# PEER stage of a decoder step: selection from 65 instead of 256 sums, lookups in one instruction per rank, and other steps for the exponentials, the gathers and the spread

## The reference, cut to what matters

```python
s = jnp.einsum('thpd,hpkd->thpk', q, keys)                 # per token and head: two rows of 128 scores
sv, si = lax.top_k(s, 16)                                  # 16 best of each row, with their places
cand = sv[:, :, 0, :, None] + sv[:, :, 1, None, :]         # 16 x 16 sums
cv, ci = lax.top_k(cand.reshape(N, 8, 256), 16)            # the 16 best sums
i1 = jnp.take_along_axis(si[:, :, 0], ci // 16, axis=-1)   # back from ranks to keys
i2 = jnp.take_along_axis(si[:, :, 1], ci % 16, axis=-1)
eidx = i1 * 128 + i2
gate = jax.nn.softmax(cv, axis=-1)
h = gelu(einsum('tkd,td->tk', u_tab[eidx], x))
out = einsum('tk,tkd->td', gate * h, v_tab[eidx])
```

## Time and profile before

| | |
|---|---|
| median of 3 runs | 2303.91 us (2300.85 to 2310.2) |
| the profiled execution | 2299.57 us, span 2297.8 us, mean granted clock 0.946 |
| PE busy | 1972.6 us, 86% |
| DVE busy | 1512.0 us, 66% |
| ACT busy | 891.1 us, 39% |
| POOL busy | 784.5 us, 34% |
| HBM | 222 GB/s over the span |

### The profile page before, as it was taken

The page is one execution under the profiler, slowest core; times in us unless marked ns, Lnnn a source line. Parts: engine busy times, 40 slices in busy tenths (PEclk is TensorE's granted clock), DMA queues, the critical chain, the costliest instruction groups (busy, mean ns, idle before and its releaser), DMA issues. The chain is left out here.

```text
span 2297.8 us, 29795 instructions
## 1 busy us (share of the span) xinstructions
PE 1972.6 (86%) x11493; PEld 1785.1 (78%) x11493; DVE 1512.0 (66%) x2468; ACT 891.1 (39%) x1752; POOL 784.5 (34%) x440
## 2 busy tenths in 40 slices
PE   4999479848898898899899998777756999998998
PEld 3998479738797697799899997666645888777876
DVE  3676444271323212492799896999966888988888
ACT  2455112111422113333444343777753334433434
POOL 0233123012531023276576776333321222222221
PEclk9999689869999999999999998999988999999999
DMA  4221100022453313256699997789889999999996
GB/s 125 65 74 40 44 1 1 5 83 83 129 202 101 129 39 114 64 173 229 250 335 337 328 328 284 270 317 346 332 345 343 397 401 402 394 401 378 396 401 244
DMA packets 211501, 513.02 MB, mean 223 GB/s; under 512 B 13216, under 2 KB 143008, under 8 KB 174496
## 3 DMA queue, kind: packets, MB, share of 16 engines
q1 hardware_dynamic: 183712, 309.77, 39.0%
q0 software_dynamic: 27648, 201.34, 22.2%
HBM read 451.26 MB, written 59.80 MB: 222 GB/s over the span
## 5 line engine op out<-in xcount | busy, mean ns | idle before, releaser
L1557 POOL TENSOR_TENSOR ex_ulo<-ex_u,ex_uhi 128x1024 fp32r<-128x1024 f32 x128 | 324.5, 2540 | 312.8 <-ACT ex_uhi L1588 310.4
L1671 PE MATMUL ps<-xhi,ex_uhi 128*128 128x384 f32 x1024 | 356.0, 348 | 24.3 <-POOL ex_ulo L1557 18.7
L1671 PE MATMUL ps<-xhi,ex_ulo 128*128 128x384 f32 x1024 | 346.3, 338 | 0.0
L1671 PE MATMUL ps<-xlo,ex_uhi 128*128 128x384 f32 x1024 | 346.3, 338 | 0.0
L1951 PE MATMUL ps<-po_vhi,po_whi 128*128 128x512 f32 x768 | 239.4, 393 | 49.9 <-DVE po_wlo L1985 49.2
L1295 POOL DMA_INDIRECT ga_ring<-in_uv,ga_idx x138 | 171.7, 1244 | 292.0 <-DVE po_acc_s L1321 175.3
L1918 ACT CAST po_vhi<-po_v 128x1024 fp32r<-128x1024 f32 x128 | 133.8, 1047 | 327.7 <-DMA po_v<-in_peer_v 291.7
L1951 PE MATMUL ps<-po_vlo,po_whi 128*128 128x512 f32 x768 | 238.5, 392 | 0.0
L1951 PE MATMUL ps<-po_vhi,po_wlo 128*128 128x512 f32 x768 | 237.7, 391 | 0.0
L1671 PEld LDWEIGHTS ps<-xhi,ex_uhi 128*128 128x128 f32 x1024 | 195.4, 191 | 29.0 <-POOL ex_ulo L1557 22.7
L1951 PEld LDWEIGHTS ps<-po_vhi,po_whi 128*128 128x128 f32 x768 | 143.8, 189 | 84.0 <-issue 54.0
(11 more groups left out here) (379 smaller groups left out, 4205.4 us busy)
## 6 DMA issues: line engine op xcount, KB each, us to landing
ex_u<-in_uT SPq DMA_DIRECT2D x128, 512.0 KB, 5.6
po_v<-in_peer_v SPq DMA_DIRECT2D x64, 1024.0 KB, 10.4
acts<-ex_h SPq DMA_DIRECT2D x64, 384.0 KB, 3.0
gates<-scores SPq DMA_DIRECT2D x12, 2048.0 KB, 7.3
po_w<-acts SPq DMA_DIRECT2D x32, 768.0 KB, 12.7
po_g<-gates SPq DMA_DIRECT2D x32, 768.0 KB, 15.8
in_w_raw<-in_w_in SPq DMA_DIRECT2D x24, 512.0 KB, 4.0
at_cache<-in_cacheT SPq DMA_DIRECT2D x6, 1024.0 KB, 5.8
```

The source lines that it names most:

```text
L1557: pool.tensor_tensor(ulo[:, j % 3], u[:, j % 3], uhi[:, j % 3].bitcast(F32), ALU.subtract).then_inc(low, 1)
L1671: mm = pe.matmul(ps[:, j % 2, 0:ND], w[:, j % 3, k, :], x[:, k, :], start=(k == 0 and n == 0), stop=(k == KT - 1 and n == 2))
```

## The change

1. `FIRST_SPREAD` goes from 104 to 85, with three quads a step instead of four: the quads lie in steps 85 to 116 instead of 104 to 127. A pick comes after every third quad.
2. Steps 117 to 126 hold 20 more picks, two a step (`LATE`). So 100 picks are done in this block instead of 96, and 104 transfers are started in it instead of 103; three more are started at once when the output block begins.
3. The exponential of the gathered rows' gates goes from step 31 to step 19, the first seven transfers from step 26 to step 13, the picks 0 to 45 to one in 4/3 of a step from step 20. Picks 46 and 47 come after the last selection, at step 84. The exponential of the dense gates goes from step 104 to step 83.
4. A selection adds only the 65 sums that can be among the 16 best, into 72 places (five small additions and a memset), and searches those. The place in the 72 is turned into two ranks by shifts and multiplications with powers of two, and a rank into a key by 16 instructions on [128 x 128] (L1768), each comparing the ranks with one number and multiplying by that rank's place, and a sum over the 16 results, which lie 128 elements apart.
5. SP's stores of gates are at step `85 + 8 * (g + 1) // 3`, before at every second step.

```diff
-FIRST_SPREAD = 104
+FIRST_SPREAD = 85
+PER_STEP = 3
-LOOP_PICKS = EARLY + 2 * (NKEY - FIRST_SPREAD)
-def early_step(n):
-    return 31 + 3 * n // 2
+LATE = 20
+LOOP_PICKS = EARLY + QUADS // PER_STEP + LATE
+def pick_step(n):
+    if n < EARLY - 2:
+        return 20 + 4 * n // 3
+    if n < EARLY:
+        return FIRST_SPREAD - 1
+    if n < LOOP_PICKS - LATE:
+        return FIRST_SPREAD + n - EARLY
+    return FIRST_SPREAD + QUADS // PER_STEP + (n - LOOP_PICKS + LATE) // 2
...
         def _(sp):
-                g = (j - FIRST_SPREAD) // 2 - 1
-                if g >= 0 and j % 2 == 0:
-                    sp.wait_ge(spread_out, NG_QUADS * (g + 1))
-                    sp.dma_start(io["gates"][g], spread[g % 2]).then_inc(spread_stored, 16)
+                for g in range(ND // 32):
+                    if j == FIRST_SPREAD + NG_QUADS * (g + 1) // PER_STEP:
+                        sp.wait_ge(spread_out, NG_QUADS * (g + 1))
+                        sp.dma_start(io["gates"][g], spread[g % 2]).then_inc(spread_stored, 16)
...
         def _(pool):
-            for n in range(LOOP_PICKS + gather.SLOTS):
+            for n in range(LOOP_PICKS + 4):
                 before = n - gather.SLOTS
...
+                step = 13 if before < 0 else pick_step(min(before + 2, LOOP_PICKS - 1)) + 1
...
         def _(act):
-                if j == early_step(0):
+                if j == pick_step(0) - 1:
                     act.wait_ge(dropped, 1)
...
-                if j == FIRST_SPREAD:
+                if j == FIRST_SPREAD - 2:
                     act.wait_ge(dropped, 2)
                     act.activation(drops[:, :], drops[:, :], ACT.Exp).then_inc(exps, 1)
+                if j == FIRST_SPREAD:
                     scale(0)
+                for x in range(PER_STEP):
+                    q = PER_STEP * (j - FIRST_SPREAD) + x
+                    if 0 < q <= QUADS:
+                        evict(q - 1)
+                    if 0 <= q < QUADS - 1:
+                        scale(q + 1)
                 for n in at.get(j, []):
                     gather.weigh(act, n)
...
         def _(pe):
-                    if k % 2 and j >= FIRST_SPREAD:
-                        quad(4 * (j - FIRST_SPREAD) + k // 2)
+                    x = PER_STEP * (j - FIRST_SPREAD) + k // 2
+                    if k in (1, 3, 5) and 0 <= x < QUADS:
+                        quad(x)
...
         def _(dve):
-                after(dve.tensor_tensor(cand[:, 0:nh, :].rearrange("p h (a b) -> p h a b", a=TOPK),
-                                        last(b4[:, :, 0, :].unsqueeze(3), TOPK), over(b4[:, :, 1, :], 2, TOPK), ALU.add))
+                dve.memset(cand[:, 0:nh, 65:SLOTS], LOWEST)
+                for a0, na, nb, c0 in ((0, 1, 16, 0), (1, 2, 8, 16), (3, 4, 4, 32), (7, 8, 2, 48), (15, 1, 1, 64)):
+                    ins = dve.tensor_tensor(cand[:, 0:nh, c0:c0 + na * nb].rearrange("p h (a b) -> p h a b", a=na),
+                                            last(b4[:, :, 0, a0:a0 + na].unsqueeze(3), nb),
+                                            over(b4[:, :, 1, 0:nb], 2, na), ALU.add)
...
-                    after(dve.tensor_tensor(eq, last(partsf[:, q, 0:nj].unsqueeze(2), TOPK), over(iota16, 1, nj),
-                                            ALU.is_equal))
-                    after(dve.tensor_tensor(e4, e4, over(wheref[:, 0:nh, q, :], 2, TOPK), ALU.mult))
-                    after(dve.tensor_reduce(out[:, q, 0:nj], eq, AX, ALU.add))
+                    for x in range(TOPK):
+                        ins = dve.scalar_tensor_tensor(out=heads_of(lookup[:, x, 0:nj]), in0=heads_of(ranks[:, q, 0:nj]),
+                                                       scalar=float(x + 1 - q), in1=last(w4[:, :, q, x:x + 1], TOPK),
+                                                       op0=ALU.is_equal, op1=ALU.mult)
+                    after(ins)
+                    after(dve.tensor_reduce(out[:, q, 0:nj], lookup[:, :, 0:nj].rearrange("p a j -> p j a"), AX, ALU.add))
...
+            for n in range(EARLY - 2, EARLY):
+                pick(n)
...
-                if q % 2:
-                    pick(EARLY + q // 2)
+                if q % PER_STEP == PER_STEP - 1:
+                    pick(EARLY + q // PER_STEP)
+            for n in range(LOOP_PICKS - LATE, LOOP_PICKS):
+                pick(n)
```

More of the change, by code:

```diff
@@ L1493, in peer_experts @@
         where = sb("where", [P, 16, TOPK], U32)
-        wheref = sb("wheref", [P, PH, 2, TOPK])
-        cand = sb("cand", [P, PH, TOPK * TOPK])
+        lookup = sb("lookup", [P, TOPK, PICKS])
         top = sb("top", [P, PH, TOPK])
         topi = sb("topi", [P, PH, TOPK], U32)
-        parts = sb("parts", [P, 2, PICKS], U32)
-        partsf = sb("partsf", [P, 2, PICKS])
+        code = sb("code", [P, 3, PICKS], U32)
+        power = sb("power", [P, 2, PICKS], U32)
+        ranks = sb("ranks", [P, 2, PICKS], U32)
         picks = sb("picks", [P, DT, 3, PICKS])
@@ L1608, in _ @@
             at = {}
-            for n in range(EARLY):
-                at.setdefault(early_step(n), []).append(n)
+            for n in range(LOOP_PICKS):
+                at.setdefault(pick_step(n), []).append(n)
             first(0)
@@ L1722, in select @@
                     ins = dve.max_index(where[:, c, 8:16], best[:, c, 8:16], s[:, c, :])
+                after(ins, True)
                 b4 = best[:, 0:2 * nh, :].rearrange("p (h q) a -> p h q a", q=2)
-                after(dve.tensor_tensor(cand[:, 0:nh, :].rearrange("p h (a b) -> p h a b", a=TOPK),
-                                        last(b4[:, :, 0, :].unsqueeze(3), TOPK), over(b4[:, :, 1, :], 2, TOPK), ALU.add))
+                dve.memset(cand[:, 0:nh, 65:SLOTS], LOWEST)
[4 more added lines that the diff above has]
+                after(ins)
                 between(3)
-                dve.tensor_copy(wheref[:, 0:nh], where[:, 0:2 * nh, :].rearrange("p (h q) a -> p h q a", q=2))
                 for c in range(nh):
@@ L1746, in select @@
                 flat = topi[:, 0:nh, :].rearrange("p h a -> p (h a)")
[L1747 to L1756 removed]
+                c3, p2 = code[:, :, 0:nj], power[:, :, 0:nj]
@@ new lines, in select @@
+                dve.tensor_scalar(c3[:, 0], flat, TOPK - 1, TOPK, ALU.bitwise_and, ALU.bitwise_or)
+                after(dve.tensor_scalar(c3[:, 1], flat, 4, None, ALU.logical_shift_right))
+                dve.tensor_scalar(p2[:, 0], c3[:, 1], 127, None, ALU.add)
+                after(dve.tensor_scalar(p2[:, 1], c3[:, 1], -1.0, 127.0, ALU.mult, ALU.add))
+                after(dve.tensor_scalar(p2, p2, 23, None, ALU.logical_shift_left))
+                after(dve.tensor_tensor(c3[:, 2], c3[:, 0], p2[:, 0].bitcast(F32), ALU.mult))
@@ new lines, in select @@
+                dve.tensor_scalar(ranks[:, 0, 0:nj], c3[:, 2], 4, None, ALU.logical_shift_right)
+                after(dve.tensor_scalar(c3[:, 1], c3[:, 2], TOPK - 1, None, ALU.bitwise_and))
+                after(dve.tensor_tensor(ranks[:, 1, 0:nj], c3[:, 1], p2[:, 1].bitcast(F32), ALU.mult))
+                heads_of = lambda ap: ap.rearrange("p (h j) -> p h j", h=nh)
+                w4 = where[:, 0:2 * nh, :].rearrange("p (h q) a -> p h q a", q=2)
+                for q in range(2):
+                    for x in range(TOPK):
+                        ins = dve.scalar_tensor_tensor(out=heads_of(lookup[:, x, 0:nj]), in0=heads_of(ranks[:, q, 0:nj]),
+                                                       scalar=float(x + 1 - q), in1=last(w4[:, :, q, x:x + 1], TOPK),
+                                                       op0=ALU.is_equal, op1=ALU.mult)
+                    after(ins)
+                    after(dve.tensor_reduce(out[:, q, 0:nj], lookup[:, :, 0:nj].rearrange("p a j -> p j a"), AX, ALU.add))
@@ L1785, in between @@
                     norm_gates(g, NPICK // TOPK, g, 1)
-                for x in range(2):
-                    pick(16 * t + 2 * i + x)
+                if t < DT - 1 or i < 7:
+                    for x in range(2):
+                        pick(16 * t + 2 * i + x)
             for t in range(DT):
@@ L1896, in _ @@
         def _(pool):
-            for n in range(LOOP_PICKS + gather.SLOTS, NPICK):
+            for n in range(LOOP_PICKS + 4, NPICK):
                 gather.fetch(pool, io, n)
```

30 lines of the change are left out of this document (4 added, 26 removed).

## The result

The changed kernel takes **2402.49 us** (median of 4 runs, 2389.26 to 2406.71) against 2306.87 us for the kernel before (4 runs, 2300.85 to 2310.2): a ratio of 1.0408, 95% interval 1.036 to 1.0455. It is slower, as forecast, but by 96 us where 27 were forecast, outside the range of 2290 to 2358. Every ratio here compares fast runs alone; one run of all_behind_less_dense was slow (2406.94 us, mean granted clock 0.812), and 2287.13 us is that kernel's median without it.

The account below looks back on a forecast made before the run. It took TensorE to bound steps before 104, DVE the spread and DMA the output block. Terms: +42 to the block's step 127, -10, -3, sum +29 on 2299.6, plus half of 4.3: 2331 us, range 2290 to 2358.

Parts of the forecast that it names:

- the ring of three engines: Spread steps: a quad passes DVE, ACT and PE in turn with two buffers, so DVE is not busy throughout; 10.2 us.
- Loads of u behind gates: Spread steps: loads issued after stores of gates land late by 0, 1.6 and 4.8 us; 10.5 us a step, 336 for 32.
- DVE's tables are then ready before POOL starts, which gives some back: Spread steps: part of the 0.8 us a step of late loads is regained, so 10.5 us a step was taken.
- A spread step: Steps with quads, walked from ACT's activation: 10.2 us before late loads; 8.7 without POOL's hold.
- Steps 0 to 84: Everything before the spread, with earlier gathers and cheaper selections: +3 us, ends -6 and +12.
- the same loss, earlier: 0: Seven gathers at once, now from step 13, delay loads of u by the same 13.1 us as before: no net change.
- Steps 117 to 127: Late steps with 20 picks: 28.2 MB at 394 GB/s, 66 us, traffic taken from the output block.
- Entry into the spread: From step 83 on, exponential, gates, two picks and copies before the first quad: 5 us over usual steps.
- -10: Block's end to the output's first load: 13 us instead of 22.9, as the last gates are stored ten steps earlier.
- -3: Output block: 88 gathers to start instead of 89, three competing with its first loads; -3 us, ends -8 and +5.
- DVE misses step 83: Slower rival, chance 0.10: dearer sums and POOL in every chain cost 28 us in three selections, less 3 slack; 2356 us.
- The chain through the two buffers does not bind: Faster rival, chance 0.15: a spread step takes 8.7 us or less, 58 us less in 32; 2273 us.

Follow-up runs that it names:

- all_behind_less_dense: Changed kernel with stores of gates and results behind loads of u, pick after a step's second quad, one pick in 3/2 step before the spread: 2287.13 us, 0.9887.
- gates_behind: The changed kernel with each store of gates moved behind the next loads of u, one semaphore per gates buffer: 2346.21 us, 1.0148.
- picks_less_dense: The changed kernel with one pick in 3/2 of a step instead of 4/3 before the spread, 44 instead of 48: 2389.68 us, 1.0366.
- all_behind_pick_middle: The changed kernel with stores of gates and of results behind loads of u, and DVE's pick after a step's second quad: 2285.95 us, 0.9904.
- selection_alone: The kernel before with the new selection alone (65 sums, one instruction per rank), every step as before: 2301.95 us, 0.997.
- before_results_behind_exp_103: The kernel before with SP's stores of results behind the next load of u and the dense gates' exponential at step 103 instead of 104: 2283.77 us, 0.9892.

## Why the prediction was wrong

The sign was right, and so were the ring of three engines and the loads behind gates. The size failed: the sum had +29 us against the profiled execution before, and the changed kernel's profiled execution is 103 longer. The 74 us between them are four terms: 27.6 in steps 85 to 116, 21.3 in steps 0 to 84, 10.2 in steps 117 to 127 and 15 behind the block.

*"Loads of u behind gates": late by 0, 1.6 and 4.8 us, 0.8 a step, net 10.5 us a step, 336.* This failed, by most of the 27.6 us between the 341 us forecast for steps 85 to 116 (with the entry) and the 368.6 measured. The 11 waits are 0.46, 1.90 and 5.04 us behind a first copy, 4.24 to 6.12 behind a second, 5.66 to 7.25 behind a third: 55.3 us, 1.75 a step. I had put the load 8.6 us behind the end of SP's wait, with 8.2 us, the fastest of the earlier trace rows, as its landing, though their median is 10.4. The one shown took 10.7, as did the median of the 11 (8.2 to 12.8). With 10.4 the same walk gives waits of 2.1, 3.8 and 7.0 us, 1.6 a step. And "DVE's tables are then ready before POOL starts, which gives some back" gave nothing back: gates_behind got 57.6 us for 55.3 us of waits. The mechanism was right, its size was not. 1.75 us a step in place of a net 0.3 are 46 us more in 32 steps, and a step of 9.6 in place of 10.2 gives 19 back: the 27 us. With them the forecast would have been 2358.

*"A spread step": 10.2 us.* Nearly right. The changed kernel shows 10.2 and 9.6 in turn, without late loads it is 9.6. That the ring and not the sum of an engine sets it was right: moving the pick to where DVE waits for PE took off another 0.95. The 10.2 shows only behind a step of another length; the walk did not have the undisturbed 9.6, and which of its offsets is 0.6 us too long is not shown.

*"Steps 0 to 84": +3, with "the same loss, earlier: 0" for the gathers.* This failed too: +24.3, of which 3.0 lie ahead of the block, 17.3 in steps 34 to 82. The burst of seven was indeed neutral (151.6 against 150.4 us in steps 1 to 33). What I never costed was the **density**: picks 0 to 45 come every 4/3 of a step instead of every 3/2. A gather of 1.05 MB each 5.55 us is 189 GB/s where each 6.24 us it is 168; with 0.52 MB of u a step (126) and 0.39 MB of results each second step (47) the demand is 362 GB/s in place of 341, and 325 and 321 were moved. Two things met. Density: picks_less_dense took back 16.7 us. And loads that SP issues only one step ahead of their use, so that any slower transfer showed: with the dense picks left as they are, all_behind_pick_middle took back 19.3. With both, 13 more went. A part comes back elsewhere: with the less dense picks DVE is later, and steps 83 and 84 take 7.4 us more (4.8 with both).

*"Steps 117 to 127": 66 us.* 76.2. The bytes were nearly right, 26.5 MB where I had 28.2, but they moved at 348 GB/s and not at the 394 of the output block. With the results stored behind the loads they moved at 384 GB/s, and with the transfers started a step sooner as well at 406.

*"Entry into the spread": 5 us over a usual step.* 16.1 less 10.2 is 5.9: right. *"-10" and "-3" behind the block* became +2 in all: the block's end took 18.2 us and not 13, and output stretches vary by some 7 us between kernels with the same code (593.2 to 600.5).

*Rivals.* "DVE misses step 83" did not happen: DVE waited 12.7 us for the exponential. But that was luck. DVE was done at 1340.9 us and not at the forecast 1323, and step 83 began at 1347.8 and not at 1326 mostly because the loads of u had delayed it. In each of the five runs of the new schedule that take 217.1 us or less for steps 34 to 82, ACT stood there for DVE, 2.6 to 9.9 us. The selections gave DVE 16.5 us (189.4 to 172.9) of the forecast 22. The rival's price for the sum over values 512 bytes apart was near: 3.82 us for 2.29, a factor of 1.67, where the rival took 2. By the Trainium skill (SBUF — State Buffer, "SBUF: two separate sides", the note on cachelines) each access that crosses to a new 16-byte line pays a penalty; the row of L1772 above agrees in kind. "The chain through the two buffers does not bind" was false as the kernel stood; with the loads mended and the pick moved, a step takes its 8.7 us.

On the change itself: before, steps 104 to 127 did the 96 quads and 48 picks in 23.2 + 260.2 = 283.4 us. The changed kernel takes 368.6 us for the same quads and 32 picks, with eight more dense steps among them, and 283.4 with every mend made here. With one pick a step DMA stands at 0.61 in the spread, and the 20 late picks come all at once, where gathers bound them. So with the mends of each (SP's order in both, the exponential at step 103 in the old, the pick's place in the new) the two schedules are level, 355.1 and 353.8 us for steps 85 to 127. A schedule with more picks in the spread and fewer behind it was not run.

## What to carry to other kernels

On a queue that issues in order, look at what stands in front of each load: a store that waits for a result of this step makes the next load a step later. Put stores behind the loads; here moving one store was worth 0.8% of the whole, and the new schedule nothing. Take a latency in a sum from the median of the rows that it will resemble, not from their least, since in this ring of engines every late load was paid in full. And an easing of one engine's rate has to be checked against what shares its queue: picks every 4/3 instead of 3/2 of a step cost 17 us where they stood, 9 of them net up to the spread.

## What was not expected of the hardware

- A chain of 16 short DVE instructions and POOL's low part get in each other's way, and by very different amounts. In the changed kernel a low part takes 4.23 us instead of 2.4 beside such a chain, and ends behind it:

```profile
1333.16 3.67 DVE L1768 SCALAR_TENSOR_TENSOR ex_lookup<-ex_ranks,ex_where 128x128 f32<-128x128 uint32 x16
```

```profile
1331.23 2.41 POOL L1566 TENSOR_TENSOR ex_ulo<-ex_u,ex_uhi 128x1024 fp32r<-128x1024 f32 x1
...
1334.85 4.23 POOL L1566 TENSOR_TENSOR ex_ulo<-ex_u,ex_uhi 128x1024 fp32r<-128x1024 f32 x1
```

In selection_alone another chain takes 10.53 us, and three low parts run within it at their usual length:

```profile
1190.30 10.53 DVE L1769 SCALAR_TENSOR_TENSOR ex_lookup<-ex_ranks,ex_where 128x128 f32<-128x128 uint32 x16
```

```profile
1190.89 2.56 POOL L1559 TENSOR_TENSOR ex_ulo<-ex_u,ex_uhi 128x1024 fp32r<-128x1024 f32 x1 [3.51 <-ACT ex_uhi L1590]
...
1194.65 2.41 POOL L1559 TENSOR_TENSOR ex_ulo<-ex_u,ex_uhi 128x1024 fp32r<-128x1024 f32 x1
1197.92 2.56 POOL L1559 TENSOR_TENSOR ex_ulo<-ex_u,ex_uhi 128x1024 fp32r<-128x1024 f32 x1 [0.86 <-ACT ex_uhi L1590]
```

The Trainium skill (SBUF — State Buffer, "SBUF: two separate sides") gives the shared ports to one instruction at a time. Which engine gets them between two instructions of a chain differs between these rows, and no run here shows what decides it.

- An exponential between other activations costs two table loads of 1.28 us beside its own 0.53 (before_results_behind_exp_103, ACT):

```profile
1404.50 1.28 ACT L1628 ACT_TABLE_LOAD   x1
1405.79 0.53 ACT L1628 ACTIVATE ex_drops<-ex_drops 128x384 f32<-128x384 f32 x1
1406.34 1.28 ACT L1619 ACT_TABLE_LOAD   x1
```
